# Twelve more projection slabs of a hybrid layer by seven block products, with VectorE writing the convolution's padded rows

## The chip, the cores and the metric

The kernel runs on one core of a Trainium2 chip. All matrices are float32. The metric is the device time of one execution in microseconds (us). The runs of the kernel before agree within 0.03%.

## The reference, cut to what matters

Two blocks of two layers each run one after the other on x, 256 tokens by 1024 channels. The change touches the first block only, in both of its layers, between the first feed-forward and the branches:

```
h = layer_norm(ALPHA * x + 0.5 * swiglu(x, ffn1_w_gu, ffn1_w_down))
(dn_q, dn_k, dn_v, dn_b, dn_a, dn_z, sw_q, sw_k, sw_v, xa_q, gates) = split(h @ w_in)
qkv  = silu(causal_depthwise_conv(concat(dn_q, dn_k, dn_v), conv_w))     # 4 taps, 1536 channels
o_dn = gated_delta_rule(q, k, v, ...) ; o_dn = rms_norm(o_dn) * silu(dn_z)
o_sw = sliding_window_attention(sw_q, sw_k, sw_v) ; o_xa = memory_cross_attention(xa_q, mem)
h = layer_norm(ALPHA * h + (sum_n sigmoid(gates_n) * (branch_n @ w_branch_n)) @ w_out)
```

The product `h @ w_in` is 256 x 1024 by 1024 x some 6,000. `gated_delta_rule` is a long chain of small steps: norms, decays, a triangular solve in six levels, a scan over four chunks.

## The kernel before, in words

**Slabs.** The weights stream from HBM through `ring`, three places of 1 MB in SBUF. SyncE fetches slab n as soon as slab n - 3 is used up (`slab_done`). A layer has 25 projection slabs, numbered w. Slabs 0 to 5 are q, k and v of the delta rule, 6 and 7 are z, 8 and 9 the queries of the cross attention, 10 and 11 those of the sliding window, 12 is half a slab for its keys, and 13 to 24 are the gates. A full slab gives 256 channels for 256 tokens.

**Slabs 0 to 12 by plain products.** `project(w)` calls `two_tiles` (L426 to L432): 16 matmuls of 128 x 128 weights by 256 tokens. A float32 matmul shows as two passes in the trace, so a slab is 32 passes of 256 columns. ScalarE then copies the bank: for w = 0 to 5 into `pad`, the rows with three leading zeros that the convolution reads (L1154), for 6 and 7 with Silu into `z` (L1178), for 8 to 11 into `xaq` and `swq` (L1186). VectorE makes the convolution of each tile of 128 channels out of `pad` in four chained operations, one TENSOR_SCALAR (L1690) and three SCALAR_TENSOR_TENSOR (L1693), two tiles a slab; ScalarE puts Silu on each (L1147).

**Slabs 13 to 24 by seven products.** `gate_half` splits the 2 x 2 blocks of weights, inputs and outputs and makes seven block products in place of eight (Strassen's method in Winograd's form): 28 matmuls of 128 columns, so 56 passes. For this GpSimd makes four sums of the inputs once a layer (`gate_input_sums`, L1987 to L1992) and four sums of each slab's weights (`gate_weight_sums`, L2014 to L2019: TENSOR_TENSOR of 128 x 512), into one of two places that take turns; from the third slab on it first waits until TensorE is done with the slab two before. TensorE makes four products into one bank (the y half) and three into another (the x half). ScalarE copies each half to SBUF (`gate_parts`, L1196 and L1202), and VectorE puts the outputs together by five additions (`gate_outputs`, L1835 to L1843). The first feed-forward already works by seven products too (L518, L531), with its weight sums made by VectorE.

**Order.** Each engine has one instruction stream, written by hand, and the engines wait for each other by semaphores. VectorE's stream after the twelve convolution tiles is the delta rule's chain: `dec_diff` (L1711), `at_beta` (L1718), the reciprocals of the norms of k and of q (L1721, L1725), the token forms, and the masks of the triangular solve (L1764 to L1775), which TensorE's first level (L792) waits for. On TensorE the small products of that chain stand between the slabs: L703 to L709 after slab 5, the sums of squares L721 after slab 7, the transposes L733 after slab 9, L747 after slab 11, and then slab 12 (L693) and L792.

## Time and profile before

| | |
|---|---|
| median of 3 runs | 3065.66 us (3065.11 to 3065.84) |
| the profiled execution's own time | 3066.11 us |
| its span in the trace | 3064.3 us |
| granted clock of TensorE over the span | 0.997 |
| layer 0, projection slab 0 to the first solve level | 249.75 to 347.04 us |
| layer 1, projection slab 0 | from 992.47 us |

Busy time is that of instructions; waiting for a semaphore is not busy. In a timeline a row has its start, its length, the engine, the kernel's line and the operation; a bracket at its end gives the idle time of the engine just before it and what ended that. A row that is longer than others of its form held its engine longer, for whatever reason. TensorE is PE, VectorE is DVE, ScalarE is ACT, GpSimd is POOL.

### The profile page before, as it was taken

The page shows a single profiled execution, that of the slowest core. Times are in us where ns is not written, and L with a number is a line of the kernel's source. Part 1 is how long each engine was busy: PE and PEld are TensorE (multiplying, and loading weights), DVE is VectorE, ACT ScalarE, POOL GpSimd, SP SyncE. Part 2 cuts the span into 40 slices and gives each one's busy share as a digit, 9 for nine tenths or more (in the row PEclk, how much of TensorE's full clock was granted, in tenths as well). Part 3 has the DMA queues.
Part 4 walks back from the last instruction along what each step waited for, and adds up shares of the span by engine and source line. Part 5 has one row for each costly group of instructions (what it writes and reads, how often), then busy time and mean ns, then how long its engine had stood idle before and what let it go on. Part 6 is the DMA issues. An engine that isn't in the chain of part 4 may idle for free.

```text
span 3064.3 us, 39414 instructions
## 1 busy us (share of the span) xinstructions
PE 2883.7 (94%) x14668; PEld 1939.3 (63%) x14668; DVE 2014.2 (66%) x4446; ACT 996.3 (33%) x2628; POOL 987.9 (32%) x664
## 2 busy tenths in 40 slices
PE   8999999999999999999999988888989998888877
PEld 8957898995995899798685433333448553333322
DVE  7753664775874656476577866666656686666665
ACT  1112231110101324021264444444445454444443
POOL 0010340000001043000013566666641256666664
PEclk9999999999999999999999999999999999999999
DMA  6544333554454333455458999999995799999998
GB/s 236 179 172 137 118 101 135 179 179 165 167 187 163 131 111 111 140 204 221 149 213 330 421 421 421 421 421 421 421 377 203 293 421 421 421 421 421 421 421 360
DMA packets 119999, 831.72 MB, mean 271 GB/s; under 512 B 13440, under 2 KB 16000, under 8 KB 21376
## 3 DMA queue, kind: packets, MB, share of 16 engines
q0 software_dynamic: 74592, 536.90, 42.2%
q1 hardware_dynamic: 43632, 282.74, 26.0%
q10 hardware_dynamic: 1584, 9.56, 0.9%
q8 instruction: 116, 1.90, 0.2%
q14 instruction: 75, 0.61, 0.1%
HBM read 828.10 MB, written 1.05 MB: 271 GB/s over the span
## 4 chain that ended last, share of the span: by engine, by line
PE 67%; DMA 15%; ACT 6%; DVE 5%; POOL 4%; issue 3%; ACTq 0%; POOLq 0%; SPq 0%; DVEq 0%
PE bank L531 12%; PE bank L2823 12%; DMA arena<-table_uv,idx 10%; PE bank L591 8%; PE bank L430 6%; DMA ring<-table_uv,idx 5%; PE bank L518 5%; PE bank L760 4%; PE bank L2503 3%; PE bank L1024 3%; POOL arena L3642 3%; PE bank L2691 2%; PE bank L457 2%; ACT diag L3101 2%; POOL ring L3642 1%
## 5 line engine op out<-in xcount | busy, mean ns | idle before, releaser
L2823 PE MATMUL bank<-arena,diag 128*128 128x512 f32 x1316 | 639.7, 612 | 99.2 <-ACT diag L3101 91.3
L3642 POOL DMA_INDIRECT arena<-table_uv,idx x324 | 490.9, 1515 | 442.0 <-issue 155.2
L3532 DVE CUSTOM_DVE_ANT_0 arena<-arena 128x1024 f32<-128x1024 f32 x330 | 403.1, 1224 | 231.7 <-DMA arena<-table_uv,idx 228.8
L2823 PEld LDWEIGHTS bank<-arena,diag 128*128 128x128 f32 x1316 | 229.6, 190 | 418.2 <-ACT diag L3101 239.7
L2823 PE MATMUL bank<-ring,diag 128*128 128x512 f32 x728 | 359.9, 620 | 60.6 <-ACT diag L3101 58.1
L2034 POOL TENSOR_TENSOR x_tok<-arena,ktail 128x1024 f32<-128x1024 f32 (+1 forms) x10 | 22.0, 2202 | 1003.5 <-ACT arena L1053 1003.5
L3642 POOL DMA_INDIRECT ring<-table_uv,idx x182 | 280.7, 1543 | 168.4 <-PE bank L2823 88.4
L3081 ACT ACTIVATE dots<-dots 128x1 f32<-128x1 f32 x512 | 103.5, 202 | 640.0 <-DVE dots L3532 635.6
L3532 DVE CUSTOM_DVE_ANT_0 ring<-ring,arena 128x1024 f32<-128x1024 f32 x182 | 222.9, 1225 | 134.5 <-DMA ring<-table_uv,idx 131.8
L2823 PEld LDWEIGHTS bank<-ring,diag 128*128 128x128 f32 x728 | 129.3, 193 | 241.3 <-ACT diag L3101 143.1
L3101 ACT ACTIVATE diag<-cst,dots 128x128 f32<-128x128 f32 x504 | 202.4, 402 | 47.8 <-PE bank L2823 1.1
L518 PE MATMUL bank<-x,ring 128*128 128x128 f32 x1408 | 173.3, 277 | 9.6 <-DMA ring<-stream 9.3
L518 PEld LDWEIGHTS bank<-x,ring 128*128 128x128 f32 x1408 | 165.8, 194 | 11.2 <-issue 8.2
L430 PE MATMUL bank<-x,ring 128*128 128x256 f32 x768 | 167.1, 379 | 0.0
L430 PEld LDWEIGHTS bank<-x,ring 128*128 128x128 f32 x768 | 145.6, 190 | 21.3 <-issue 1.9
L3098 ACT ACTIVATE dots<-dots,soft 128x1 f32<-128x1 f32 x504 | 148.4, 294 | 16.2
L2503 PE MATMUL bank<-xn,ring 128*128 128x256 f32 x448 | 99.4, 380 | 0.0
L2014 POOL TENSOR_TENSOR pad<-ring 128x512 f32<-128x512 f32 x12 | 15.2, 1269 | 251.4 <-DMA ring<-stream 197.2
L2503 PEld LDWEIGHTS bank<-xn,ring 128*128 128x128 f32 x448 | 84.6, 190 | 14.3 <-issue 3.2
L591 PE MATMUL bank<-ring,hid 128*128 128x512 f32 x184 | 86.7, 592 | 0.0
L531 PE MATMUL bank<-Q,ring 128*128 128x128 f32 x528 | 70.0, 276 | 0.6 <-DVE X L1414 0.4
L531 PEld LDWEIGHTS bank<-Q,ring 128*128 128x128 f32 x528 | 64.2, 192 | 1.1 <-DVE X L1414 0.8
(747 smaller groups left out, 5013.6 us busy)
## 6 DMA issues: line engine op xcount, KB each, us to landing
ring<-stream SPq DMA_DIRECT2D x238, 1024.0 KB, 4.9
ktail<-ln_rows ACTq DMA_DIRECT2D x6, 1024.0 KB, 5.0
arena<-stream SPq DMA_DIRECT2D x6, 1024.0 KB, 9.8
arena<-table_uv,idx POOLq DMA_INDIRECT x336, 20.6
ring<-table_uv,idx POOLq DMA_INDIRECT x182
arena<-mem_rows SPq DMA_DIRECT2D x2, 1024.0 KB, 9.8
more<-stream SPq DMA_DIRECT2D x2, 1024.0 KB, 8.5
cst<-stream SPq DMA_DIRECT2D x2, 1024.0 KB, 7.7
```

The costliest lines, as they stand in the source:

```text
L430: last = mm(out[:, half * T:half * T + T], w[:, half * KC + k, :], rhs[:, k, :], start=(k == 0), stop=(k == KC - 1))
L518: mm(out[:, lo:lo + P], w[:, at_k + k, :], x[:, at_k + k, 0:P], start=(k == 0), stop=(k == KC // 2 - 1))
L531: last = mm(out, weights[:, k, :], rhs[:, k, :], start=(k == 0), stop=(k == KC // 2 - 1))
L591: return mm(bank[W_ACC[i]][:, :], lhs, rhs, start=(w == 0), stop=(w == DOWN_SLABS - 1))
L760: last = mm(bank[b][:, n * P:n * P + P], weights[k], rhs[:, k, :], start=(k == 0), stop=(k == KC // 2 - 1))
L2503: last = mm(out_[:, half * T:half * T + T], w[:, half * KC + k, :], rhs[:, k, :], start=(k == 0), stop=(k == KC - 1))
L2823: last = mm(bank[4 + 2 * tt + half][:, :], diag[:, n % DIAGS, :], row_slot(l, n)[:, D + 512 * half:D + 512 * half + 512], start=(h == 0 an ...
L3081: value = fn(dots[:, tt, k:k + 1], dots[:, tt, k:k + 1], ACT.Gelu)
L3098: step.did(fn(dots[:, tt, k:k + 1], dots[:, tt, k:k + 1], ACT.Copy, scale=soft[:, h % 2, tt, k:k + 1]))
L3101: fn(diag[:, n % DIAGS, :], c_("ident"), ACT.Copy, scale=dots[:, tt, k:k + 1]).then_inc(diag_ready.sem, 1)
L3532: v.tensor_tensor_reduce(u, u, tok[:, tt, :], 1.0, 0.0, ALU.mult, ALU.add, dots[:, tt, k:k + 1]).then_inc(u_used.sem, 1)
L3642: g.indirect_dma_start(out=row_slot(l, n), out_offset=None, in_=peer_uv, in_offset=number).then_inc(row_loaded[PLACE[l][n]], 16)
```

## The change

All twelve full slabs 0 to 11 of each layer go by seven products too, and only slab 12 stays as it was. On TensorE `project(w)` calls `seven_y` and `seven_x`. GpSimd's weight sums run over all 24 slabs of `SEVENS` in order, after the input sums. ScalarE makes two copies a slab into a scratch part of `hid`, and VectorE puts the outputs together (`seven_outputs`), for slabs 0 to 5 straight into `pad`. Silu on z becomes one operation of its own.

```diff
-STREAM_BANK = [w % BANKS for w in range(GATES_FROM)]
-GATE_X, GATE_Y = 0, 1
+SEVENS = tuple(range(SW_SLAB)) + tuple(range(GATES_FROM, WIN_SLABS))
+SEVEN_X = 0
+SEVEN_Y = {w: 1 + w % 2 if w < SW_SLAB else 1 for w in SEVENS}
```

On TensorE:

```diff
+                def seven_y(w):
+                    slab(l, WIN_AT + w)
+                    pe.wait_ge(t_ready.sem, t_ready.at(l, W_SLABS + SEVENS.index(w) + 1))
+                    b, use = stream_use(w)
+                    pe.wait_ge(stream_free[b].sem, stream_free[b].at(l, use))
+                    seven_product(b, 1, seven_sum(w, 1), gate_x_sums[:, 0])
+                    seven_product(b, 0, seven_sum(w, 3), gate_x_sums[:, 2])
+                    seven_product(b, 2, seven_sum(w, 4), x[:, KC // 2:KC, P:T])
+                    seven_product(b, 3, own_blocks(w, 3 * KC // 2), gate_x_sums[:, 3]).then_inc(gu_done.sem, 1)
+                def seven_x(w):
+                    b, use = stream_use(w, 1)
+                    pe.wait_ge(stream_free[b].sem, stream_free[b].at(l, use))
+                    seven_product(b, 2, seven_sum(w, 2), gate_x_sums[:, 1])
+                    seven_product(b, 0, own_blocks(w, 0), x[:, 0:KC // 2, 0:P])
+                    seven_product(b, 1, own_blocks(w, KC // 2), x[:, KC // 2:KC, 0:P]).then_inc(slab_done.sem, 1)
                 def project(w):
-                    if w != SW_SLAB:
-                        two_tiles(out, weights, x).then_inc(slab_done.sem, 1)
-                        return
+                    if w in SEVENS:
+                        seven_y(w)
+                        seven_x(w)
+                        return
```

On ScalarE:

```diff
                 for w in range(6):
-                    evac_done(fn(pad[:, w % 3, :, CONV_TAPS - 1:], src[:, :].rearrange("p (a t) -> p a t", a=2),
-                                 ACT.Copy), w)
+                    seven_y(w)
+                    seven_x(w)
...
+                seven_y(6)
                 for tt in range(TT):
                     act.wait_ge(dec_diff.sem, dec_diff.at(l, tt + 1))
                     fn(qdec[:, tt].rearrange("p h c -> p (h c)"), bank[3 + tt][:, :],
                        ACT.Exp).then_inc(qdec_exp.sem, 1)
+                seven_x(6)
...
```

On VectorE, where the calls for slabs 6 and 7 come behind `at_beta`, that for 8 ahead of the reciprocal of q's norms, 9 behind the token forms, 10 ahead of L1764, and 11 ahead of the second solve level:

```diff
+                def seven_outputs(w):
+                    for second in range(2):
+                        b, use = stream_use(w, second)
+                        dve.wait_ge(stream_free[b].sem, stream_free[b].at(l, use + 1))
+                    block = [seven_part(w, n, n + 1)[:, 0, :] for n in range(7)]
+                    first, middle, last = seven_rows(w)
+                    step.did(v.tensor_tensor(first, block[0], block[1], ALU.add))
+                    step.did(v.tensor_tensor(block[2], block[0], block[2], ALU.add))
+                    step.join()
+                    step.did(v.tensor_tensor(seven_part(w, 0, 2), block[2].unsqueeze(1).broadcast_to([P, 2, P]),
+                                             seven_part(w, 3, 5), ALU.add))
+                    step.join()
+                    step.did(v.tensor_tensor(last, block[0], block[4], ALU.add))
+                    v.tensor_tensor(middle, seven_part(w, 0, 2), seven_part(w, 5, 7), ALU.add).then_inc(gu_summed.sem, 1)
                 for t in range(3 * HEADS):
                     w = t // 2
-                    dve.wait_ge(stream_free[w % BANKS].sem, stream_free[w % BANKS].at(l, w // BANKS + 1))
+                    if t % 2 == 0:
+                        seven_outputs(w)
+                        step.join()
+                        dve.wait_ge(gu_summed.sem, gu_summed.at(l, FC + SEVENS.index(w) + 1))
...
+                seven_outputs(6)
+                seven_outputs(7)
+                seven_outputs(8)
+                seven_outputs(9)
+                seven_outputs(10)
+                seven_outputs(11)
```

On GpSimd:

```diff
-                        for j in range(GATE_SLABS):
-                            gate_weight_sums(l, j)
+                        for w in SEVENS:
+                            seven_weight_sums(l, w)
```

VectorE's stream where the convolution starts, before the change (`pad` and `conv` are the padded rows and the tile's result):

```order
L1678 TENSOR_TENSOR Y<-cst,tiny 128x512
L1690 TENSOR_SCALAR conv<-pad,prm 128x256
L1693 SCALAR_TENSOR_TENSOR conv<-pad,prm,conv 128x256 x3
L1690 TENSOR_SCALAR conv<-pad,prm 128x256
L1693 SCALAR_TENSOR_TENSOR conv<-pad,prm,conv 128x256 x3
```

The same place in the changed kernel, where `hid` as a source is the scratch part that ScalarE's copies fill:

```order
L1718 TENSOR_TENSOR Y<-cst,tiny 128x512
L1730 TENSOR_TENSOR pad<-hid 128x128
L1731 TENSOR_TENSOR hid<-hid 128x128
L1733 TENSOR_TENSOR hid<-hid 128x256
L1736 TENSOR_TENSOR pad<-hid 128x128
L1737 TENSOR_TENSOR pad<-hid 128x2x128
L1749 TENSOR_SCALAR conv<-pad,prm 128x256
L1752 SCALAR_TENSOR_TENSOR conv<-pad,prm,conv 128x256 x3
L1749 TENSOR_SCALAR conv<-pad,prm 128x256
L1752 SCALAR_TENSOR_TENSOR conv<-pad,prm,conv 128x256 x3
```

Five additions now stand ahead of the two tiles of each slab, and nothing of what stood there has gone.

ScalarE's stream in the changed kernel between the squares and the square roots, where L1186 and L1191 are the copies of a slab's y and x halves:

```order
L1218 ACT_TABLE_LOAD
L1218 ACTIVATE tiny<-gsm 128x8
L1219 ACTIVATE tiny<-tiny 128x8
L1220 ACTIVATE egl<-gsm 128x16
L1186 ACTIVATE hid<-bank 128x512
L1224 ACTIVATE qdec<-bank 128x512 x2
L1191 ACTIVATE hid<-bank 128x384
L1230 ACTIVATE dec<-dec 128x256 x2
L1186 ACTIVATE hid<-bank 128x512
L1191 ACTIVATE hid<-bank 128x384
L1235 ACT_TABLE_LOAD
L1235 ACTIVATE arena<-bank,eps 128x512 x4
```

Before, no copy of a slab stood between these exponentials; now the x half of slab 6 is copied behind the two that wait for `dec_diff`, and TensorE's x half of slab 7 waits for that copy.

## Rows read from the trace of the kernel before

**Rows 1.** The page, busy time of each engine.
```profile
PE 2883.7 (94%) x14668; PEld 1939.3 (63%) x14668; DVE 2014.2 (66%) x4446; ACT 996.3 (33%) x2628; POOL 987.9 (32%) x664
```

**Rows 2.** Timeline of TensorE, layer 0: start us, us, what; x counts passes.
```profile
249.75 41.60 PE L430 MATMUL bank<-x,ring 128*128 128x256 f32 x192
...
294.66 13.98 PE L430 MATMUL bank<-x,ring 128*128 128x256 f32 x64
...
347.04 1.15 PE L792 MATMUL bank<-cst,lt 64*64 64x64 f32 x32
```

**Rows 3.** Timeline of TensorE, seven-product slabs of layer 1's first feed-forward.
```profile
788.37 1.95 PE L518 MATMUL bank<-x,ring 128*128 128x128 f32 x16
...
794.62 1.95 PE L518 MATMUL bank<-x,ring 128*128 128x128 f32 x16
```

**Rows 4.** Timeline of VectorE, layer 0, from the first convolution tile.
```profile
257.83 0.35 DVE L1690 TENSOR_SCALAR conv<-pad,prm 128x256 f32<-128x256 f32 x1
...
260.04 1.53 DVE L1693 SCALAR_TENSOR_TENSOR conv<-pad,prm,conv 128x256 f32<-128x256 f32 x3
...
294.61 1.53 DVE L1693 SCALAR_TENSOR_TENSOR conv<-pad,prm,conv 128x256 f32<-128x256 f32 x3
...
296.36 5.01 DVE L1711 SCALAR_TENSOR_TENSOR dec<-bank,gsm,cst 64x64 f32<-64x64 f32 x16
302.64 0.69 DVE L1718 TENSOR_TENSOR at_<-dec,bank 128x512 f32<-128x512 f32 x1 [1.27 <-ACT dec L1176]
311.88 6.55 DVE L1721 RECIPROCAL arena<-arena 128x1024 f32<-128x1024 f32 x1 [8.55 <-ACT arena L1182]
...
342.57 0.69 DVE L1764 TENSOR_TENSOR at_<-at_,bank 128x512 f32<-128x512 f32 x1 [8.72 <-PE bank L747]
```

**Rows 5.** Timeline of VectorE, the five additions of gate slab 13.
```profile
363.52 0.29 DVE L1835 TENSOR_TENSOR hid<-qT 128x128 f32<-128x128 f32 x1
...
364.72 0.42 DVE L1843 TENSOR_TENSOR hid<-qT 128x256 f32<-128x256 f32 x1
```

**Rows 6.** Timeline of GpSimd, weight sums of gate slabs.
```profile
346.21 1.75 POOL L2014 TENSOR_TENSOR hid<-ring 128x512 f32<-128x512 f32 x1 [1.45 <-DMA ring<-stream]
...
369.25 1.27 POOL L2014 TENSOR_TENSOR hid<-ring 128x512 f32<-128x512 f32 x1 [6.45 <-PE bank L760]
...
373.17 1.26 POOL L2019 TENSOR_TENSOR hid<-ring,hid 128x512 f32<-128x512 f32 x1
...
404.47 1.24 POOL L2017 TENSOR_TENSOR pad<-ring,pad 128x512 f32<-128x512 f32 x1
405.79 1.18 POOL L2019 TENSOR_TENSOR conv<-ring,pad 128x512 f32<-128x512 f32 x1
```

**Rows 7.** Timeline of VectorE beside three of those GpSimd rows.
```profile
346.15 0.68 DVE L1775 TENSOR_TENSOR lt<-at_,cst 128x512 f32<-128x512 f32 x1
346.87 1.64 DVE L1783 TENSOR_TENSOR Y<-cst,lt 128x512 f32<-128x512 f32 x1
...
404.37 0.29 DVE L1835 TENSOR_TENSOR hid<-qT 128x128 f32<-128x128 f32 x1
404.58 1.27 DVE L1836 TENSOR_TENSOR qT<-qT 128x128 f32<-128x128 f32 x1
405.89 1.36 DVE L1838 TENSOR_TENSOR qT<-qT 128x256 f32<-128x256 f32 x1
```

**Rows 8.** Timeline of GpSimd, last input sum of layer 0.
```profile
232.81 1.26 POOL L1992 TENSOR_TENSOR gate_x_sums<-x,gate_x_sums 128x512 f32<-128x512 f32 x1
```

**Rows 9.** Timeline of GpSimd, last input sum of layer 1.
```profile
989.34 1.27 POOL L1992 TENSOR_TENSOR gate_x_sums<-x,gate_x_sums 128x512 f32<-128x512 f32 x1
```

**Rows 10.** Timeline of TensorE, layer 1, first six projection slabs.
```profile
992.47 41.60 PE L430 MATMUL bank<-x,ring 128*128 128x256 f32 x192
```

**Rows 11.** Timeline of VectorE, layer 1, first convolution operation.
```profile
1000.55 0.35 DVE L1690 TENSOR_SCALAR conv<-pad,prm 128x256 f32<-128x256 f32 x1
```

**Rows 12.** The page, DMA issues: KB each, us from issue to landing.
```profile
ring<-stream SPq DMA_DIRECT2D x238, 1024.0 KB, 4.9
```

**Rows 13.** Timeline of TensorE, its first passes.
```profile
8.27 3.75 PE L518 MATMUL bank<-x,ring 128*128 128x128 f32 x16 [8.27 <-DMA ring<-stream]
```

More of the change, by code:

```diff
@@ L42, with stream_use @@
 SW_SLAB = 12
-STREAM_BANK = [w % BANKS for w in range(GATES_FROM)]
-STREAM_USE = [STREAM_BANK[:w].count(STREAM_BANK[w]) for w in range(GATES_FROM)]
-GATE_SLABS = WIN_SLABS - GATES_FROM
-GATE_X, GATE_Y = 0, 1
+SEVENS = tuple(range(SW_SLAB)) + tuple(range(GATES_FROM, WIN_SLABS))
+SEVEN_X = 0
+SEVEN_Y = {w: 1 + w % 2 if w < SW_SLAB else 1 for w in SEVENS}
+STREAM_BANK = [b for w in range(WIN_SLABS) for b in ((SEVEN_Y[w], SEVEN_X) if w in SEVENS else (w % BANKS,))]
+STREAM_AT = [w + sum(u < w for u in SEVENS) for w in range(WIN_SLABS)]
+def stream_use(w, second=0):
+    at = STREAM_AT[w] + second
+    return STREAM_BANK[at], STREAM_BANK[:at].count(STREAM_BANK[at])
 GATE_OWN = 6
@@ L256, in weight_sum, with seven_sum_rows @@
             return space[(q - 1) // 2][:, (q - 1) % 2 * HALF:(q - 1) % 2 * HALF + HALF]
-        def gate_sum(j, q):
-            if j % 2 == 0:
-                if q == 4:
-                    flat = conv[:, :, :].rearrange("p a t -> p (a t)")
-                    return [flat[:, k * P:k * P + P] for k in range(KC // 2)]
-                return [pad[:, q - 1, k // 2, CONV_TAPS - 1 + k % 2 * P:CONV_TAPS - 1 + k % 2 * P + P] for k in range(KC // 2)]
-            flat = gate_sum_rows(j, q)
-            return [flat[:, k * P:k * P + P] for k in range(KC // 2)]
-        def gate_sum_rows(j, q):
-            if j % 2 == 0:
+        def seven_sum_rows(w, q):
+            if w > SW_SLAB and w % 2 == 1:
                 if q == 4:
@@ L338, in first_block @@
         ba_done = sig("ba_done", 1)
[L339 removed]
+        stream_free = [sig(f"stream_free{b}", STREAM_BANK.count(b)) for b in range(BANKS)]
         conv_done = sig("conv_done", 12)
[L341 removed]
+        silu_done = sig("silu_done", 13)
         beta_ready, a_exp, a_ln = in_turn("ba_by_act", 1, 1, 1)
@@ L678, in tensor, with seven_product, own_blocks @@
                 last.then_inc(ba_done.sem, 1)
+                def seven_product(b, n, weights, rhs):
+                    for k in range(KC // 2):
+                        last = mm(bank[b][:, n * P:n * P + P], weights[k], rhs[:, k, :], start=(k == 0), stop=(k == KC // 2 - 1))
+                    return last
+                def own_blocks(w, at):
+                    return [ring[:, (WIN_AT + w) % RING, at + k, :] for k in range(KC // 2)]
+                def seven_y(w):
+                    slab(l, WIN_AT + w)
+                    if w < 2:
+                        pe.wait_ge(mem_evac.sem, mem_evac.at(l, 4))
+                    pe.wait_ge(t_ready.sem, t_ready.at(l, W_SLABS + SEVENS.index(w) + 1))
[5 more added lines that the diff above has]
+                    seven_product(b, 3, own_blocks(w, 3 * KC // 2), gate_x_sums[:, 3]).then_inc(gu_done.sem, 1)
@@ L1176, in scalar @@
                     fn(half, half, ACT.Exp).then_inc(dec_exp.sem, 1)
-                for w in (6, 7):
-                    evac_done(fn(z[:, 2 * (w - 6):2 * (w - 6) + 2, :].rearrange("p h t -> p (h t)"),
-                                 projected(w)[:, :], ACT.Silu), w)
+                seven_y(7)
+                seven_x(7)
                 for i in range(4):
@@ L1950, in vector @@
                 step.join()
+                dve.wait_ge(silu_done.sem, silu_done.at(l, 13))
                 v.tensor_tensor(flat_o, flat_o, z[:, :, :].rearrange("p h t -> p (h t)"), ALU.mult).then_inc(o_ready.sem, 1)
-                for j in range(9, GATE_SLABS):
-                    gate_outputs(j)
+                for w in SEVENS[-3:]:
+                    seven_outputs(w)
                 for r in range(3 * KC):
```

162 lines of the change are left out of this document (77 added, 85 removed).

## The prediction

> **What bounds the kernel now.** I read the page first, then the timelines of layer 0 from the first projection slab to the first level of the triangular solve. TensorE is busy 94% of the span [rows 1], and in this stretch it never stops: six slabs take 41.6 us and the next row begins as they end, so a plain slab costs 6.91 us (41.44 / 6) [rows 2]. VectorE is less busy, 66% [rows 1], but its chain is the one to watch. A slab's two convolution tiles take it from 257.83 to 261.5, which is 3.66 us; the last tile ends at 296.1; then come the decays (L1711), `at_beta` (L1718), and only twice does it wait long for TensorE, 8.55 us before the first reciprocal and 8.72 us before L1764 [rows 4]. TensorE's first solve level at 347.04 [rows 2] comes right behind the masks that VectorE makes there. So TensorE bounds this stretch, and VectorE follows with some 3 us of slack a slab (6.91 - 3.66) and 17 us in the rest.
>
> **What the change takes off TensorE.** A seven-product slab at full pace takes 6.25 us, from 788.37 to 794.62 [rows 3]. Each of twelve slabs a layer saves 6.91 - 6.25 = 0.66 us, 7.9 us a layer, 15.8 us in all. That is the most that it can give.
>
> **What it puts on the others, taken alone.**
> - GpSimd: four weight sums a slab, 369.25 to 374.43, 5.2 us [rows 6]. Each slab's sums start when TensorE is done with the slab two before; TensorE then has 6.25 us of other work, so they fit if they stay near 5.2. Fetches fit as well: a slab lands 4.9 us after its issue [rows 12] and is fetched three slabs ahead.
> - Start of a layer: the input sums end at 234.1 in layer 0, over 15 us before slab 0 [rows 8, 2], so nothing is late. In layer 1 they end at 990.6 [rows 9]; with 5.2 us for slab 0's sums TensorE can begin at 995.8 in place of 992.47 [rows 10], 3.3 us late.
> - ScalarE: two copies a slab for one. It is 33% busy [rows 1]; I cost this at nothing, hidden under TensorE's 6.25 us.
> - VectorE: five additions a slab, 363.52 to 365.14, about 1.65 us with the wait behind them [rows 5]. With the tiles that is 5.3 us a slab, still under 6.25.
>
> Added up like this the change is a gain. The next point is what I think turns it.
>
> **VectorE and GpSimd hold each other up.** In the gate stage they run TENSOR_TENSOR side by side, and whichever comes second stands. A mask product that takes 0.68 us takes 1.64 us when issued at 346.87, inside a weight sum that itself took 1.75 us for 1.27 [rows 7, 6]. In one set of gate additions the second took 1.27 us, where 0.29 is the first's length, and the third 1.36 us for 0.42, beside the weight sums of 404.47 and 405.79 [rows 7, 5, 6]. In numbers: a GpSimd sum that meets a waiting addition costs VectorE about 1.0 us (1.27 - 0.29 = 0.98, 1.36 - 0.42 = 0.94), and the two take turns. Before the change GpSimd does nothing while the convolution runs, its sums begin at the gates. After it GpSimd is at work there 5.2 of every 6.25 us.
>
> The convolution's three SCALAR_TENSOR_TENSOR a tile read two operands from SBUF (`pad` and `conv`), as the additions do, but no row has one beside a GpSimd sum. Bounds for them: from nothing, as if they passed freely, to the 1.0 us of an addition. I take the upper, since they are nearest in form to the rows that were held: same engine, float32, two SBUF operands.
> The Trainium skill's page "SBUF — State Buffer", section "Who interferes with whom", says that a VectorE instruction with two SBUF inputs and a GpSimd instruction that reads SBUF exclude each other for the whole instruction. By that rule the convolution's operations are held too; the additions in the rows above agree with it, and the convolution is not shown by any row of before. By the same section a TENSOR_SCALAR between two SBUF tiles may be held as well, which no row shows.
>
> **The sum, layer 0.** Over slabs 0 to 5 VectorE needs 6 x 5.3 = 31.8 us alone. While it does them GpSimd makes the sums of slabs 2 to 7, 24 operations. If VectorE always has a two-operand operation ready, each costs it 1.0 us: 31.8 + 24 = 56 us, or 9.3 us a slab, more than TensorE's 6.25 and than the 6.91 of before. The loop begins at 257.8 as before, so the last tile ends at 313.8 in place of 296.1: 17.8 us late. TensorE can't run away from this: ScalarE's y copy of slab w waits for the outputs of slab w - 2, and stands behind the Silu of the tiles before it, so TensorE is throttled two to three slabs ahead of VectorE.
>
> The rest of the chain, from the last tile to L792, was 347.04 - 296.1 = 50.9 us [rows 2, 4]. It gains outputs 6 to 10, 5 x 1.65 = 8.2 us alone, and GpSimd's remaining 20 or so operations there meet VectorE about half the time (the two reciprocals of 6.55 us read one operand), some 9 us more: 17 us. Against that stand the 8.55 and 8.72 us of idle [rows 4], 17.3 us, since TensorE has that much fewer plain slabs left between its own steps and waits now itself. The first of these idles can't vanish wholly: slab 7's x half waits for slab 6's copy behind `dec_diff` (5.3 us after the loop), then 2.7 us of products, L721 and the roots follow; but outputs 6 and 7 fill that time. So the rest keeps its length to about 1 us, and layer 0 ends 17.8 us later. Layer 1 has the same and a later start: slab 0 done at 995.8 + 6.25 = 1002.1, its copies about 0.9 us later, 1003.0 in place of 1000.55 [rows 11]: 2.5 us more, 20.3 us.
>
> Behind the first level I see nothing that gives it back or adds much: the gates work as before, and outputs 11 fall in a wait. So 17.8 + 20.3 = 38.1 us on the profiled execution's own 3066.1 us (span 3064.3): **3104 us**. The median of before is 0.45 us below that execution, which is nothing here.
>
> **The rivals.**
> 1. Only the additions are held, the convolution passes. Of five additions two or three meet a sum; at 2.7 a slab the loop takes 6 x 8.0 = 48 us, the last tile ends at 305.8, 9.7 us late. With layer 1's 2.5: 2 x 9.7 + 2.5 = 22 us, 3088 us. For it: no row shows the convolution's operation held. Against: it reads two SBUF operands too.
> 2. It gets faster: additions and sums miss each other, and VectorE stays at 5.3 us a slab. TensorE gains 7.9 us in layer 0 and 7.9 - 3.3 = 4.6 in layer 1: 12.5 us, 3053.6 us. It decides from the point where VectorE's slab is under 6.91 us, so held by less than 1.6 us a slab. Against: the weight sums of slab w + 2 start when slab w is done, and so do the copies and additions of slab w, so the two meet by construction.
> 3. It ends about where it was: holds of some 1.6 us a slab, the break-even just named. I know no reason for that size.
> 4. More than the forecast: TensorE stands up to 13 us at a time, above all before slab 7's x half. After the 8.27 us of idle at the start of the program its first sixteen passes took 3.75 us for 1.95 [rows 13, 3], so a stop can cost 1.8 us (3.75 - 1.95) or more, most of it while VectorE is behind anyway. Were the tiles' first operations (L1690) held too, little would be added, since the sum already has all 24 GpSimd operations met; I allow 2 us a layer. With two stops of 1.8 us showing, 3104 + 4 + 4 = 3112 us.
>
> **The numbers.** Chances: 0.52 for the forecast with what rival 4 adds, 0.30 for rival 1, 0.12 for faster, 0.06 for about the same. A measurement of this kernel tells 0.2%, about 6 us, from no change. Slower by more than that: 0.84, within it 0.05, faster 0.11. For eight in ten the range must hold the forecast and rival 1 with their slack: from 3076 (rival 1 with two additions held: 6 x 7.3 = 44 us, 5.5 us late, 3066.1 + 11 + 2.5 = 3079.6, less 3 for the estimate of the rest) to 3112.
>
> **What would show it.** In the changed kernel's trace the convolution's SCALAR_TENSOR_TENSOR (L1752) should average well over the 0.5 us of before (1.53 for three [rows 4]), near 0.9, with single ones at 1.4; the additions at L1730 to L1737 near 1.0 where unheld ones are 0.29; GpSimd's sums at 1.3 to 1.5; the six-slab loop at 56 us on VectorE; idle time of TensorE in this stretch of 25 to 30 us a layer, released through ScalarE's copies. If L1752 stays at 0.5 us, rival 1 holds; if TensorE has no idle time there, rival 2. I would be wrong from the ground up if operations of the two engines overlapped freely here, or if the rest of the chain took the delay in.

## The result, and the profile after

The changed kernel takes 3125.26 us (median of 4 runs, 3123.23 to 3127.07), beside 3065.39 us of the kernel before in the same comparison (4 runs, 3062.96 to 3065.84). The ratio is 1.0198, with a 95% interval of 1.0182 to 1.0214: about 60 us slower. The forecast was 3104 us within 3076 to 3112. The forecast had the right sign, and the measured time lies outside its range.

The page first, its busy times and two groups of TensorE (group rows: busy us, mean ns | idle us just before, and what ended most of it):

```profile
PE 2890.8 (93%) x15244; PEld 1962.5 (63%) x15244; DVE 2128.0 (68%) x4566; ACT 1009.9 (32%) x2654; POOL 1114.2 (36%) x760
...
L708 PE MATMUL bank<-gate_x_sums,hid 128*128 128x128 f32 x720 | 98.2, 289 | 39.8 <-ACT hid L1191 36.0
...
L708 PE MATMUL bank<-x,ring 128*128 128x128 f32 x768 | 99.5, 286 | 0.0
```

Beside [rows 1] VectorE is busy 114 us more (2128.0 - 2014.2) and GpSimd 126 us more (1114.2 - 987.9). TensorE is busy no less, 2890.8 us for 2883.7, though the change took multiplications off it: the seven-product passes of the two groups take 289 and 286 ns (275 in run 1, further on, where TensorE hardly stops), and it now stands 39.8 us in the first of them, nearly all of it for ScalarE's copy of an x half (L1191).

VectorE, layer 0, from the first addition on. L1730 and its neighbours are additions, L1749 and L1752 the convolution (L1690 and L1693 before), L1770 the decays (L1711 before), L1782 and L1787 the reciprocals:

```profile
259.66 1.35 DVE L1730 TENSOR_TENSOR pad<-hid 128x128 f32<-128x128 f32 x1
...
276.29 0.35 DVE L1749 TENSOR_SCALAR conv<-pad,prm 128x256 f32<-128x256 f32 x1
276.68 1.52 DVE L1752 SCALAR_TENSOR_TENSOR conv<-pad,prm,conv 128x256 f32<-128x256 f32 x3
...
286.16 4.19 DVE L1752 SCALAR_TENSOR_TENSOR conv<-pad,prm,conv 128x256 f32<-128x256 f32 x3
290.27 1.35 DVE L1749 TENSOR_SCALAR conv<-pad,prm 128x256 f32<-128x256 f32 x1
...
316.82 5.00 DVE L1770 SCALAR_TENSOR_TENSOR dec<-bank,gsm,cst 64x64 f32<-64x64 f32 x16
...
328.00 0.93 DVE L1730 TENSOR_TENSOR z<-hid 128x128 f32<-128x128 f32 x1 [2.32 <-ACT hid L1191]
...
333.23 6.54 DVE L1782 RECIPROCAL arena<-arena 128x1024 f32<-128x1024 f32 x1
339.80 2.34 DVE L1784 TENSOR_TENSOR kT<-kT,arena 128x1024 f32<-128x1024 f32 x1
...
346.57 6.54 DVE L1787 RECIPROCAL arena<-arena 128x1024 f32<-128x1024 f32 x1
```

GpSimd in the same stretch:

```profile
279.67 1.50 POOL L2067 TENSOR_TENSOR hid<-ring 128x512 f32<-128x512 f32 x1 [4.95 <-PE bank L708]
...
285.92 1.33 POOL L2067 TENSOR_TENSOR hid<-ring 128x512 f32<-128x512 f32 x1 [0.73 <-PE bank L708]
287.21 1.45 POOL L2068 TENSOR_TENSOR hid<-ring 128x512 f32<-128x512 f32 x1
288.74 1.33 POOL L2070 TENSOR_TENSOR hid<-ring,hid 128x512 f32<-128x512 f32 x1
290.14 1.33 POOL L2072 TENSOR_TENSOR hid<-ring,hid 128x512 f32<-128x512 f32 x1
```

The reader is to lay the two side by side. At 276.68 GpSimd stands idle (its 4.95 us before 279.67), and three passes of the convolution take 1.52 us, as in [rows 4]. At 286.16 it is in its sums, and the same three take 4.19 us: 0.9 us more each. The TENSOR_SCALAR behind them takes 1.35 us for 0.35 as the fourth sum ends. Grouped by line over the loop:

```profile
L1752 DVE SCALAR_TENSOR_TENSOR conv<-pad,prm,conv 128x256 f32<-128x256 f32 x36 | 29.2, 812 | 1.3
L1749 DVE TENSOR_SCALAR conv<-pad,prm 128x256 f32<-128x256 f32 x12 | 7.9, 655 | 0.6
```

TensorE, layer 0, around and behind the loop, with its stops in brackets (L747 is slab 12, L824 the first solve level, L792 before):

```profile
322.89 2.08 PE L708 MATMUL bank<-gate_x_sums,hid 128*128 128x128 f32 x8 [10.06 <-ACT hid L1191]
...
363.80 5.32 PE L747 MATMUL bank<-x,ring 128*128 128x256 f32 x16 [3.56 <-ACT hid L1191]
...
372.40 1.15 PE L824 MATMUL bank<-cst,lt 64*64 64x64 f32 x32 [3.28 <-DVE lt L1839]
```

The first level comes at 372.40 for 347.04 [rows 2]. From the small projection's end to there TensorE stands 25.4 us in layer 0 and 30.5 in layer 1, 21.3 and 21.6 of them for ScalarE's copies. Layer 1 begins with TensorE waiting for GpSimd's first sums, and VectorE's smallest operations are held there as well:

```profile
1023.20 3.76 PE L708 MATMUL bank<-gate_x_sums,hid 128*128 128x128 f32 x16 [3.46 <-POOL hid L2072]
1026.74 1.91 PE L708 MATMUL bank<-x,hid 128*128 128x128 f32 x8
...
1032.43 1.95 PE L708 MATMUL bank<-gate_x_sums,hid 128*128 128x128 f32 x16
```

```profile
1024.22 1.19 DVE L1680 TENSOR_SCALAR tiny<-tiny 128x8 f32<-128x8 f32 x1
1025.45 0.17 DVE L1682 TENSOR_SCALAR tiny<-tiny 128x8 f32<-128x8 f32 x1
...
1033.22 0.93 DVE L1730 TENSOR_TENSOR pad<-hid 128x128 f32<-128x128 f32 x1 [2.11 <-ACT hid L1191]
```

Windows of the changed kernel (busy us and count of PE, PEld, DVE, ACT, POOL; then TensorE's granted clock, DMA share, GB/s):

```profile
257.00:316.00 59.00, 47.80 (x372) 45.63 (x370) 56.77 (x79) 10.52 (x22) 37.49 (x28) 0.91 0.35 124
312.00:327.00 15.00, 4.93 (x31) 4.75 (x30) 11.31 (x30) 7.46 (x15) 2.73 (x3) 0.66 0.10 40
1015.00:1019.00 4.00, 4.00 (x31) 3.52 (x30) 0.00 (x0) 1.08 (x2) 3.77 (x4) 1.00 0.45 137
1019.00:1032.00 13.00, 9.54 (x60) 9.37 (x59) 7.60 (x16) 5.62 (x10) 8.78 (x8) 0.74 0.10 40
```

In the loop VectorE is busy 56.77 of 59 us: it sets the pace, and TensorE works 47.80. Its granted clock is 1.00 at 1015 to 1019, and 0.74 in the window that holds the 3.46 us stop: within it, 0.50 from 1023 to 1029, the lower of the two levels.

The table measures each stretch from the end of TensorE's small projection (L676 before, L701 after) to the first solve level, in each kernel's own trace. "Loop" is VectorE from its first addition or convolution operation to the first decay; "start" is what lies ahead of that and "rest" what lies behind it.

| kernel, layer | start | loop | rest | together |
|---|---|---|---|---|
| before, 0 | 7.9 | 38.5 | 50.7 | 97.1 |
| before, 1 | 7.9 | 38.5 | 50.7 | 97.1 |
| changed, 0 | 10.1 | 57.2 | 55.6 | 122.8 |
| changed, 1 | 13.5 | 59.6 | 56.5 | 129.6 |

So +25.7 us in layer 0 and +32.4 in layer 1, 58.1 of the 60.3 us between the two spans (3124.6 and 3064.3). The other 2.2 us lie outside these stretches. Right behind the first level TensorE's passes are longer for a few microseconds, so that the second level comes 1.7 us later after the first in layer 0 and 3.0 in layer 1; what follows in layer 1 gives part of that back.

### The profile page after: what moved, and what is told of

It reads as the page before. It is cut to its first block, busy times and chain, and to the rows that moved or that the text cites. A ratio compares the mean times of both kernels' runs of the same rounds, so it can differ in the third digit from the quotient of the medians.

```text
span 3124.6 us, 40872 instructions
## 1 busy us (share of the span) xinstructions
PE 2890.8 (93%) x15244; PEld 1962.5 (63%) x15244; DVE 2128.0 (68%) x4566; ACT 1009.9 (32%) x2654; POOL 1114.2 (36%) x760
## 4 chain that ended last, share of the span: by engine, by line
PE 34%; DMA 15%; ACT 5%; DVE 5%; issue 3%; POOL 3%; ACTq 0%; POOLq 0%; DVEq 0%
PE bank L2876 13%; DMA arena<-table_uv,idx 12%; DMA ring<-table_uv,idx 4%; PE bank L2556 3%; PE bank L556 3%; PE bank L708 2%; PE bank L616 2%; ACT diag L3154 2%; POOL arena L3695 2%; PE bank L2744 1%; PE bank L1058 1%; PE bank L543 1%; DVE arena L3585 1%; PE bank L2591 1%; PE bank L482 1%
## 5 line engine op out<-in xcount | busy, mean ns | idle before, releaser
L543 PE MATMUL bank<-x,ring 128*128 128x128 f32 x1408 | 173.3, 277 | 9.7 <-DMA ring<-stream 9.5
L543 PEld LDWEIGHTS bank<-x,ring 128*128 128x128 f32 x1408 | 165.8, 194 | 11.3 <-issue 8.4
L708 PE MATMUL bank<-gate_x_sums,hid 128*128 128x128 f32 x720 | 98.2, 289 | 39.8 <-ACT hid L1191 36.0
L708 PEld LDWEIGHTS bank<-gate_x_sums,hid 128*128 128x128 f32 x720 | 91.8, 203 | 44.3 <-ACT hid L1191 37.2
L708 PE MATMUL bank<-x,ring 128*128 128x128 f32 x768 | 99.5, 286 | 0.0
L708 PEld LDWEIGHTS bank<-x,ring 128*128 128x128 f32 x768 | 95.8, 203 | 0.0
L2067 POOL TENSOR_TENSOR hid<-ring 128x512 f32<-128x512 f32 x30 | 39.8, 1327 | 117.1 <-PE bank L708 108.9
```

What stands on the lines that cost most here:

```text
L543: mm(out[:, lo:lo + P], w[:, at_k + k, :], x[:, at_k + k, 0:P], start=(k == 0), stop=(k == KC // 2 - 1))
L708: last = mm(bank[b][:, n * P:n * P + P], weights[k], rhs[:, k, :], start=(k == 0), stop=(k == KC // 2 - 1))
L2067: step.did(g.tensor_tensor(t1, b12, b11, ALU.subtract))
```

## The experiments

The runs are numbered in the order in which they were made, since their expectations name each other by it, and are told here in the order of the argument. The line numbers in the rows are each kernel's own. Slabs 0 to 11 are "the twelve slabs".

**Run 1: are the sums the cause at all?** This kernel forms 8 of each weight sum's 512 columns and feeds rows of the slab to the products in their place, so the first block's projections are not the reference's. All waits and all other operations stay.

```diff
+                if w < SW_SLAB:
+                    t1, t2, t3, t4, b11, b21, b12, b22 = (u[:, 0:POOL_EDGE] for u in (t1, t2, t3, t4, b11, b21, b12, b22))
-                    seven_product(b, 1, seven_sum(w, 1), gate_x_sums[:, 0])
+                    seven_product(b, 1, product_sum(w, 1), gate_x_sums[:, 0])
...
+                    return own_blocks(w, q % 4 * KC // 2) if w < SW_SLAB else seven_sum(w, q)
```

> The weight sums of the twelve slabs are cut to 8 of their 512 columns on GpSimd, and the matrix products of those slabs read rows of the slab instead of the sums, so the first block's projections are not the reference's; every VectorE addition, every hand-off and every product stays. Theory A (VectorE's and GpSimd's operations hold each other up in SBUF): VectorE's loop over slabs 0-5 needs only its unheld 31.8 us and falls back to the pace of the products, about 37.5 us a layer, layer 1's start loses its extra wait, the outputs 6-11 hide; near 3053.6, between 3050 and 3062. Theory B (the additions and the chain TensorE, ScalarE, VectorE, TensorE cost by themselves, the sums little): the stops of the products stay, 3090 or more. Theory C (TensorE's lower clock is its own cause): the granted clock stays at 0.6 to 0.8 in the loop and the time above 3080.

Measured: 3049.22 us (3047.68 to 3050.70), ratio 0.9953 [0.9936, 0.9970]: 14 us faster than before and 76 us faster than the changed kernel, a little below theory A's lower end. The groups by line, and a window, of this kernel:

```profile
L1755 DVE SCALAR_TENSOR_TENSOR conv<-pad,prm,conv 128x256 f32<-128x256 f32 x36 | 17.4, 485 | 1.3
L1752 DVE TENSOR_SCALAR conv<-pad,prm 128x256 f32<-128x256 f32 x12 | 4.2, 351 | 0.6
```

```profile
257.00:293.00 36.00, 36.00 (x308) 34.57 (x307) 30.73 (x79) 10.29 (x22) 5.50 (x23) 1.00 0.50 173
```

The same operations take 485 and 351 ns instead of 812 and 655. In this window TensorE never stops, and its clock is at 1.00. The loop takes 35.9 us in both layers, a seven-product slab's pace. Theories B (the chain and additions themselves) and C (the clock as a cause of its own) fall: both effects exist only where the sums do. That holds behind the loop too: with every addition in place the rest is 46.8 and 45.6 us, shorter than before the change (50.7) and 8.8 and 10.9 us under the changed kernel's.

**Run 2: the sums without the additions.** The twelve slabs as full products as before, but GpSimd forms their sums into space that nobody reads, and each slab's products wait for them.

```diff
-SEVENS = tuple(range(SW_SLAB)) + tuple(range(GATES_FROM, WIN_SLABS))
+SEVENS = () + tuple(range(GATES_FROM, WIN_SLABS))
+SUMMED = (0, 1, 2, 3, 4, 5, 6, 7, 8, 9, 10, 11) + tuple(range(GATES_FROM, WIN_SLABS))
...
+                    if w in SUMMED:
+                        pe.wait_ge(t_ready.sem, t_ready.at(l, W_SLABS + SUMMED.index(w) + 1))
```

> The full products of before for slabs 0-11, ScalarE writing the padded rows, no addition on VectorE; but GpSimd forms the four sums of each slab into space that nobody reads, and each slab's products wait for them. Theory A: the convolution's own passes over the accumulator are held too; its loop needs about 22 us unheld plus 24 sums of about 1.1 us, near 49 us for the 38.5 of before, so +8 to +10 us a layer, and layer 1 starts 3 to 4 us later: 3082 to 3092. Rival (my prediction's lesser case: only the new additions are held): the loop keeps its 38.5 us and only layer 1's first slab waits: 3066 to 3072.

Measured: 3128.41 us, ratio 1.0209 [1.0192, 1.0226], and neither theory had that. The trace shows why it can't be used as a whole: my generalised wait for reused space made the weight sums of gate slabs 20, 22 and 24 wait for the slab just before. TensorE stops there, in a part that the change doesn't touch:

```profile
447.23 3.75 PE L709 MATMUL bank<-gate_x_sums,pad 128*128 128x128 f32 x16 [2.70 <-issue]
...
466.75 2.04 PE L709 MATMUL bank<-gate_x_sums,kbe 128*128 128x128 f32 x8 [8.47 <-issue]
```

Ahead of that, layer 0 is sound; the next run has the whole.

**Run 5 (mended run 2).**

```diff
...
-                if same and same[-1] not in SUMMED[max(0, n - 2):n - 1] and w not in (GATES_FROM + GATE_OWN, ):
+                if same and SUMMED.index(same[-1]) > n - 2:
```

> As the second run (sums formed, full products, nobody reads the sums), but without the wait that I had put on GpSimd by mistake: there each weight sum of gate slabs 20, 22 and 24 waited for the slab just before it, which stopped TensorE by up to 8.5 us at four places in layer 0 behind the part under study. What that run showed ahead of them stands: the loop of slabs 0-5 took 44.4 us for 38.5 and the first level began 1.4 us later in layer 0; in layer 1 slab 0 waited 3.5 us and the loop began some 2 us later still. Theory (held passes of the convolution hide behind the products' 41.6 us and the chain's idles, apart from their ends): 3068 to 3075. If the sums alone cost what the change costs: above 3100.

Measured: 3071.11 us (3070.69 to 3075.04), ratio 1.0026 [1.0015, 1.0037]: 7 us slower than before, inside the theory's range. The convolution's groups, and the two rows of VectorE that waited 8.55 and 8.72 us in [rows 4]:

```profile
L1786 DVE SCALAR_TENSOR_TENSOR conv<-pad,prm,conv 128x256 f32<-128x256 f32 x36 | 33.9, 942 | 1.3
L1783 DVE TENSOR_SCALAR conv<-pad,prm 128x256 f32<-128x256 f32 x12 | 10.2, 852 | 0.0
```

```profile
315.46 6.55 DVE L1816 RECIPROCAL arena<-arena 128x1024 f32<-128x1024 f32 x1 [4.29 <-ACT arena L1260]
...
343.72 0.69 DVE L1862 TENSOR_TENSOR at_<-at_,bank 128x512 f32<-128x512 f32 x1 [4.10 <-PE bank L809]
```

This settles the point that no row of before could: the convolution's own passes are held, 942 ns for 0.5 us, and its TENSOR_SCALAR too. The loop grows to 45.6 us in each layer, 7.1 more than before (it was 45.6 in run 2's layer 0 too, where the expectation has 44.4). And yet the rest shrinks from 50.7 to 44.0 us, because the two idles fall to 4.29 and 4.10: the chain takes the loop's delay in almost wholly, all but 0.4 us a layer; the later starts, 1.1 and 3.4 us, remain. Holds alone are cheap here, as additions alone are in run 1; the change pays because both draw on the same idle time.

**Run 3: take VectorE's second SBUF operand away, in the convolution.** The changed kernel with the accumulator in PSUM, the memory that holds TensorE's banks; one product of the decay row moves behind slab 6 to make room.

```diff
-                    src, acc = pad[:, w % 3, t % 2, :], conv[:, t % 2, :]
+                    src, acc = pad[:, w % 3, t % 2, :], bank[5 + t % 2][:, 0:T]
...
-                mm(bank[5][:, :], c_("same_chunk"), betac, start=True, stop=True).then_inc(grow_done.sem, 1)
                 project(6)
+                pe.wait_ge(silu_done.sem, silu_done.at(l, 11))
+                mm(bank[5][:, :], c_("same_chunk"), betac, start=True, stop=True).then_inc(grow_done.sem, 1)
```

> The changed kernel, but the convolution's accumulator lies in PSUM banks 5 and 6, so each of its passes reads one operand from SBUF and one from PSUM; the same result. If only VectorE operations with two operands in SBUF are held: the 18 accumulating passes of three slabs go at unheld lengths beside the sums, only the additions and reciprocals meet, the loop of slabs 0-5 falls from 57 and 59 to 40 to 46 us a layer; 3088 to 3100. If anything that VectorE reads or writes in SBUF beside GpSimd is held: no gain, 3118 to 3130. PSUM reads could also be dearer by themselves (some 0.1 us a pass, 14 us in all).

Measured: 3104.04 us, ratio 1.0132 [1.0116, 1.0149]: 21 us back, for one operand moved, though 4 us above the range that I expected. The moved product is part of this and of the later kernels with PSUM operands; run 7 shows that it costs nothing that counts there. The loops fall from 57.2 and 59.6 to 49.5 and 49.7 us, above the 40 to 46 that I expected, since the additions now meet the sums that the convolution met before: layer 0's thirty additions take 25.6 us for 19.4 in the changed kernel, and their middle one averages 1.38 us.

```profile
L1753 DVE SCALAR_TENSOR_TENSOR bank<-pad,prm,bank 128x256 f32<-128x256 f32 x36 | 17.6, 490 | 1.3
L1734 DVE TENSOR_TENSOR hid<-hid 128x256 f32<-128x256 f32 x6 | 8.3, 1382 | 0.2
```

**Run 4: and in the additions of slabs 0 to 5.** ScalarE copies one product of seven, and VectorE's additions take the other six from PSUM.

```diff
+                        step.did(v.tensor_tensor(first, block[0], out_x[:, P:2 * P], ALU.add))
+                        v.tensor_tensor(block[2], block[0], out_x[:, 2 * P:3 * P], ALU.add).then_inc(free.sem, 1)
...
+                        step.did(v.tensor_tensor(seven_part(w, 0, 2), block[2].unsqueeze(1).broadcast_to([P, 2, P]),
+                                                 out_y[:, 0:2 * P].rearrange("p (b t) -> p b t", t=P), ALU.add))
...
+                        fn(seven_part(w, 0, 1).rearrange("p b t -> p (b t)"), bank[SEVEN_X][:, 0:P],
+                           ACT.Copy).then_inc(stream_free[SEVEN_X].sem, 1)
```

> As the run before, and in slabs 0-5 ScalarE copies only one of the seven products (128 columns); VectorE's five additions take the other six directly from PSUM, so none has two operands in SBUF. The same result. If the two-operand rule holds: VectorE's loop is not held at all and goes at the pace of the products, 37 to 42 us; what is left is layer 1's start (about 5 us), the additions of slabs 6-11 and the held reciprocals: 3070 to 3088. Rival: bank 0 now comes free only behind VectorE's additions, and the products stop for them: the loop stays above 46 us and the time above 3095.

Measured: 3080.12 us (3079.03 to 3083.44), ratio 1.0055 [1.0038, 1.0071]: another 24 us back. VectorE's groups of this kernel in the loop, and two of GpSimd's sums beside them:

```profile
L1785 DVE SCALAR_TENSOR_TENSOR bank<-pad,prm,bank 128x256 f32<-128x256 f32 x36 | 17.6, 490 | 1.3
L1782 DVE TENSOR_SCALAR bank<-pad,prm 128x256 f32<-128x256 f32 x12 | 5.8, 485 | 0.6
L1751 DVE TENSOR_TENSOR hid<-hid,bank 128x256 f32<-128x256 f32 x6 | 2.5, 422 | 0.4 <-DVE hid L1748 0.3
```

```profile
263.88 1.27 POOL L2100 TENSOR_TENSOR hid<-ring 128x512 f32<-128x512 f32 x1 [1.06 <-PE bank L711]
265.11 1.28 POOL L2101 TENSOR_TENSOR hid<-ring 128x512 f32<-128x512 f32 x1
```

With GpSimd's sums running all through the loop no VectorE operation in it is longer than when alone, and layer 1's sums take 1.26 to 1.28 us. (The TENSOR_SCALAR takes 480 to 489 ns in run 7 as well, whose first tiles have no sum beside them.) The loops take 34.8 and 37.5 us, less than before the change. The Trainium skill's page "SBUF — State Buffer", section "Who interferes with whom", says that a VectorE instruction with at most one SBUF input, outside its two-port modes, does not contend with GpSimd. By that rule the trace agrees, for TENSOR_TENSOR, SCALAR_TENSOR_TENSOR and a TENSOR_SCALAR that writes PSUM. The rival, that TensorE stops for bank 0, falls too: it stops once in layer 0's loop, for 0.78 us, and not in layer 1's. What is left above the kernel before lies behind the loop, where the rest is 55.2 and 54.6 us (4.5 and 3.9 more), and at the starts, which are 10.1 and 12.0 us (2.2 and 4.0 more); the additions of slabs 6 to 11 still read two operands from SBUF here, and no run moves those.

**Run 10: one edit on the chain behind the loop of the changed kernel.**

```diff
-                seven_outputs(8)
                 dve.wait_ge(l2_std.sem, l2_std.at(l, 4))
...
                                        ALU.mult).then_inc(kq_ready.sem, 1)
+                seven_outputs(8)
```

> The changed kernel, with VectorE's additions of slab 8 moved from between the two reciprocals to behind qT's product. My prediction held the chain behind the loop at its length; it grew by 5 to 6 us a layer, and the additions of slab 8 stand in it for 4.5 us. Theory A (it was this place: the transposes and the score products come late by it): 4 us a layer back, 3116 to 3119. Theory B (VectorE itself is now busy from the first reciprocal to the first level, so its additions cost the same wherever they stand): 3122 to 3127.

Measured: 3126.25 us (3124.36 to 3127.67), ratio 1.0201 [1.0185, 1.0217]: no gain over the changed kernel's 3125.26, as theory B said. In layer 0 the stretch is 1.9 us shorter (120.9 for 122.8 us), in layer 1 0.5, and the whole shows nothing. Where these additions stand matters little; that VectorE has them to do, with the holds that they meet, is what costs.

**Run 9: the changed kernel, slab 0 by full products.**

```diff
-SEVENS = tuple(range(SW_SLAB)) + tuple(range(GATES_FROM, WIN_SLABS))
+SEVENS = (1, 2, 3, 4, 5, 6, 7, 8, 9, 10, 11) + tuple(range(GATES_FROM, WIN_SLABS))
```

> The changed kernel, with slab 0 of both layers by full products, copied by ScalarE, as before the change; nothing else. My prediction gave layer 1's later start 2.5 us. The trace of the changed kernel shows 5.6 us of it: TensorE idle for GpSimd's first sums, then slab 0 at a granted clock of 0.74. Theory: both go, and with them slab 0's additions (2 to 6 us in each loop) and its share of sums: layer 1 gives back 7 to 10 us, layer 0 some 2 to 4; 3112 to 3117. Rival: the loop is bound by meeting sums wherever it starts, so only the start comes back: 3119 to 3121.

Measured: 3112.19 us (3111.02 to 3117.99), ratio 1.0161 [1.0144, 1.0177]: 13 us back for one slab of twelve, 9.3 in layer 1's stretch and 3.8 in layer 0's. The size lies at the lower end of the theory's, and the places are somewhat other: layer 1's start gives back only 2.2 us (11.3 for 13.5), because VectorE's small operations are still held by the sums of slab 1, and its loop 6.2 us (53.4 for 59.6).

**Runs 6, 7, 8, 11 and 12: towards a version that beats both.** All have the PSUM operands of run 4 and differ in which slabs go by seven products; the others take the path of the kernel before. Run 8 also moves slab 8's additions as in run 10. The edit is the tuple:

```diff
-SEVENS = tuple(range(SW_SLAB)) + tuple(range(GATES_FROM, WIN_SLABS))
+SEVENS = (1, 2, 3, 4, 5) + tuple(range(GATES_FROM, WIN_SLABS))
```

(run 7; in the others the slabs that the table names).

Run 6, slabs 0 to 5. 

> Seven products for slabs 0-5 alone, VectorE's additions and the convolution's accumulator in PSUM as in the fourth run, slabs 6-11 as full products evacuated by ScalarE as before the change; the same result. If the rest of the fourth run's excess lies in VectorE's chain behind the loop (outputs 6 to 10, about 20 us a layer, where the chain had 17 us of idle time): the first level begins 3 to 4 us a layer earlier than in the kernel before, less layer 1's late start of 5 to 6: 3056 to 3064. Rival (TensorE's products of slabs 6-12 then set the end and give the gain back, or the late decay row, whose product I put behind slab 6, costs): 3064 to 3075.

Run 8, slabs 1 to 11. 

> The fourth run with slab 0 by full products and VectorE's additions of slab 8 moved behind both reciprocals. Against the 3080 of the fourth run: layer 1's start gives back 4 us, and the move about 4.5 us a layer if the transposes and the first score products are then not late: 3066 to 3073. Rival: VectorE's chain behind the loop is busy from end to end, so moved additions cost what they cost before: 3074 to 3078.

Run 7, slabs 1 to 5. 

> As the run beside it, but slab 0 by full products too, so that no product waits for GpSimd's first sums at the head of layer 1. If that wait (3.5 us) and TensorE's lower clock behind it (2 us) are the price of layer 1's start: 4 to 5 us below the run beside it in layer 1, less 0.7 us a layer for the longer product: 3 to 4 us less in all, 3053 to 3061. If the clock and the wait have another cause: the same as beside it, plus 1.

Run 11, slabs 1 to 7. 

> The seventh run's kernel (3058.5) with slabs 6 and 7 by seven products too, ScalarE copying their parts and VectorE adding them where it waits for the first square roots (an idle of 7.3 us a layer in the seventh run's trace). Theory: TensorE is the bound there, VectorE's additions (2 and 5 us, the second held by sums) fit into that idle time and into the 8.7 us behind the transposes, and two slabs save 0.66 us each a layer: 2.6 us less, 3055.5 to 3057. Rival (the hand-offs to ScalarE stop TensorE, as they did for slab 7 in the changed kernel, or the additions outgrow the idle time): 3059 to 3065.

Run 12, slabs 1 to 7, 9 and 10. 

> As the run beside it, with slabs 9 and 10 by seven products as well; their additions stand where VectorE waits 8.7 us for the score products in the seventh run's trace. They take 3.6 to 4.7 us each when sums hold them, so 8.3 us in an idle time that shrinks to about 6 as TensorE gets faster by 0.66 us a slab. If the idle time is just used up: 3053 to 3056, the least of all. If VectorE's chain becomes the bound there: 3057 to 3062, above the run beside it. I take the second as likelier, since the kernel with slabs 1 to 11 took 3070.

| run | slabs by seven | median us | ratio to before | stretch, layers 0 and 1 |
|---|---|---|---|---|
| before | none | 3064.5, 3064.3, 3063.7 (three comparisons) | | 97.1, 97.1 |
| 4 | 0 to 11 | 3080.12 | 1.0055 [1.0038, 1.0071] | 100.0, 104.1 |
| 8 | 1 to 11 | 3070.15 | 1.0021 [1.0012, 1.0031] | 98.8, 96.9 |
| 6 | 0 to 5 | 3064.61 | 1.0002 [0.9993, 1.0011] | 96.4, 98.3 |
| 7 | 1 to 5 | 3058.47 | 0.9981 [0.9972, 0.9990] | 93.9, 93.9 |
| 11 | 1 to 7 | 3058.00 | 0.9979 [0.9969, 0.9988] | 92.6, 92.6 |
| 12 | 1 to 7, 9, 10 | 3056.48 | 0.9975 [0.9965, 0.9984] | 92.4, 92.4 |

Run 6 came out even with before, just above its theory's 3056 to 3064 and in its rival's range. In layer 1 it has the 3.5 us stop and a slower slab 0. In layer 0 two sums of gate slabs, from 342.42 and 343.89, meet the masks ahead of the first level; VectorE of run 6:

```profile
341.92 2.56 DVE L1902 TENSOR_TENSOR qdec<-qdec,qT 128x512 f32<-128x512 f32 x2
344.40 1.75 DVE L1906 TENSOR_TENSOR lt<-at_,cst 128x512 f32<-128x512 f32 x1
```

These take 1.29 and 0.68 us when alone. Run 7 has neither, and its 3058.47 us lie in the theory's range, though the gain over run 6 is 6 us and not 3 to 4. Its VectorE has both long waits, and TensorE never stops in the stretch:

```profile
308.04 6.55 DVE L1849 RECIPROCAL arena<-arena 128x1024 f32<-128x1024 f32 x1 [7.30 <-ACT arena L1275]
...
338.74 0.69 DVE L1895 TENSOR_TENSOR at_<-at_,bank 128x512 f32<-128x512 f32 x1 [8.72 <-PE bank L816]
```

So the stretch is worth what TensorE saves: 5 slabs x 0.66 = 3.3 us a layer, and 97.1 - 93.9 = 3.2 are found. That is TensorE's saving, at the size that the prediction gave it. Run 11 spends the first of the two idles (0.89 us are left of it), run 12 both. In run 12 neither row has an idle time before it; of VectorE:

```profile
310.36 6.54 DVE L1852 RECIPROCAL arena<-arena 128x1024 f32<-128x1024 f32 x1
...
337.32 0.67 DVE L1898 TENSOR_TENSOR at_<-at_,bank 128x512 f32<-128x512 f32 x1
```

Nine slabs would save 5.9 us a layer; 4.7 are found, with one stop of TensorE of 0.89 us a layer, so both engines are now near their limit. Run 11 fell between its two ranges, and so did run 12; that run 12 would be the slower of them, as I took for likelier, is not borne out. The intervals of runs 7, 11 and 12 overlap, so their order isn't shown; that each is faster than before is, by 0.2% to 0.25% (6 to 8 us). Run 8 shows the limit from the other side: with all of slabs 1 to 11 the stretches are back at 98.8 and 96.9 us. Its time lies in its theory's range, but not for the theory's reason: of the 4.5 us a layer that moving slab 8's additions was to give, the rest shows at most 0.9 and 2.2 (54.3 and 52.4 for run 4's 55.2 and 54.6), as in run 10. The hit is partly luck.

## Why the prediction was right in sign and wrong in size

**TensorE's saving, right.** 0.66 us a slab was the size. Runs 7 and 11 deliver it: 3.2 and 4.5 us a layer for 5 and 7 slabs (3.3 and 4.6 worked out).

**The mechanism, right.** VectorE and GpSimd hold each other up. Run 1 takes the sums away and 76 us go, run 4 takes the second SBUF operand away and every duration in the loop returns to its unheld length with the sums still running. TensorE stands 25.4 and 30.5 us a layer, mostly for ScalarE's copies, where I named 25 to 30. Rival 2, faster by additions and sums that miss each other, is what run 1 looks like (3049.2 for the 3053.6 worked out).

**The convolution, right.** I priced its passes by the additions, with no row for it. Run 5 shows them held at 942 ns for 0.5 us. Rival 1 (only the additions held) is out.

**The six-slab loop, nearly right.** 56 us forecast, 57.2 and 59.6 found (38.5 before), so +18.7 us for +17.8 in layer 0, and +21.1 in layer 1. The shares are not as named: L1752 averages 0.81 us for 0.9, the additions 0.65 us in layer 0 and 0.77 in layer 1 for near 1.0, and what I had left out at the tiles' first operation (L1749, 0.66 us for 0.35) makes up for part of it. That the total fits so well is in part luck. GpSimd's sums, in the rows above, take 1.33 to 1.50 us, as forecast. Layer 1's excess over layer 0 comes with its slab 0: run 9, which has that slab by full products, takes 6.2 us off layer 1's loop and 3.2 off layer 0's, and the two are then 53.4 and 54.0.

**The step that failed: "So the rest keeps its length to about 1 us".** It grew from 50.7 to 55.6 and 56.5 us, 4.9 and 5.8 a layer. I had set 17 us of additions and holds against 17.3 us of idle. In layer 0's trace outputs 6 to 10 take about 1.7, 5.2, 4.5, 3.1 and 4.6 us, and kT's product 1.1 more than alone: 20 us, 3 above the estimate. The additions alone are the 8.2 us that I had, so the term that I sized too small is the holds, 12 us for 9. And 2.3 us of idle stay before outputs 7 (the row at 328.00), where ScalarE's copy of slab 7's x half comes late; I had named that wait and counted it as filled. Run 1 shows that the additions by themselves fit into the idle time (rest 46.8 and 45.6 us); run 10 shows that it isn't the place of one set that costs. Run 5 shows the idle time was real and does absorb holds; it can be spent only once.

**The start of a layer, wrong.** Layer 0's loop begins 2.2 us later in its stretch, which I had at nothing: the three products ahead of it (L1717 and L1718) are held by the sums of slab 2, 4.1 us for 2.0. In layer 1 I had 2.5 us and found 5.6. The stop of 3.3 us was right (3.46), but slab 0's products then took 9.2 us instead of 6.25 (1023.20 to 1032.43), the first half of them at the lower granted clock. I had the clock's cost as a rival, 1.8 us for a stop, in the belief that it falls where VectorE is behind anyway. Here TensorE is what VectorE waits for (the 2.11 us before 1033.22).

Together: 0.9 + 3.3 us in the loops, 4.9 + 5.8 in the rest, 2.2 + 3.1 at the starts, and 2.2 outside the stretches are 22.4 us, which but for rounding is the distance between the 38.1 us forecast and the 60.3 found. The range's upper end of 3112 left 8 us for all of these terms. They went the same way, and most, as I read them, have one cause: I charged holds and stops only to the operations I had counted, not to what stood around them.

## What to carry to other kernels

When GpSimd work is added beside a VectorE chain, look at each VectorE operation's operands, the small ones and those already there too: in this kernel two operands in SBUF cost 0.9 to 1.0 us for each sum met, while the same operation with one operand in PSUM cost nothing. Spend an engine's idle time in the books once, as run 5 against the changed kernel shows. And when a change saves a little on the bounding engine for work on another, apply it to just so many tiles as the other's idle time pays for: with the PSUM operands, five to nine of the twelve slabs, without slab 0, gained 0.2% to 0.25% and eleven or twelve lost 0.2% to 0.6%.
